# The first two pairs of weight tiles of the input projection: smaller loads from two queues, and a new order of the products

## The reference, cut to what matters

```python
    proj = jnp.einsum('btd,dc->btc', x, w_in) + b_in
    q, k, v, glu = jnp.split(proj, [ATTN_WIDTH, ATTN_WIDTH + KV_WIDTH, ATTN_WIDTH + 2 * KV_WIDTH], axis=-1)
    ...
    attn, new_k, new_v = attend_fn(q, k, v)
    a, g = jnp.split(glu, 2, axis=-1)
    c, new_conv = causal_dwconv(conv_hist, a * jax.nn.sigmoid(g), conv_w, conv_b)
    c = jax.nn.silu(layer_norm(c, conv_ln_g, conv_ln_b))
    mix = jnp.einsum('btm,md->btd', jnp.concatenate([attn, c], axis=-1), w_out) + b_out
    x = layer_norm(ALPHA * x + mix, ln1_g, ln1_b)
    h = jnp.einsum('btd,df->btf', x, ffn_w_up)
    h, new_ffn = causal_dwconv(ffn_hist, h, ffn_conv_w, ffn_conv_b)
    hu, hg = jnp.split(h, 2, axis=-1)
    f = jnp.einsum('btf,fd->btd', jax.nn.silu(hg) * hu, ffn_w_down)
    x = layer_norm(ALPHA * x + f, ln2_g, ln2_b)
```

## Time and profile before

| | us |
|---|---|
| median of 3 runs | 2038.24 |
| lowest, highest | 2037.86, 2039.66 |
| the profiled execution, its own time | 2040.65 |
| its span | 2039.1 |
| TensorE busy in the span | 1992.8 (98%) |
| first real product starts | 8.47 |
| second pair ends, first q product starts | 38.30 |

### The profile page before, as it was taken

The page is one execution under the profiler, slowest core; times in us unless marked ns, Lnnn a source line. Parts: engine busy times, 40 slices in busy tenths (PEclk is TensorE's granted clock), DMA queues, the critical chain, the costliest instruction groups (busy, mean ns, idle before and its releaser), DMA issues. The chain is left out here.

```text
span 2039.1 us, 42519 instructions
## 1 busy us (share of the span) xinstructions
PE 1992.8 (98%) x15699; PEld 1971.7 (97%) x15699; DVE 1660.6 (81%) x2619; ACT 990.4 (49%) x1503; POOL 408.0 (20%) x557
## 2 busy tenths in 40 slices
PE   8999999999998999999999999999999999999996
PEld 8999999899988999999999999999999999999995
DVE  3599899977699777777777777777778889899898
ACT  3445444433566454444444444444446545454445
POOL 0022223120642211111111121111211121112212
PEclk9999999999999999999999999999999999999997
DMA  6322222123657767667677676776766898779973
GB/s 223 99 78 78 84 88 77 51 81 127 204 156 217 206 180 187 181 183 194 176 186 191 177 191 175 185 191 176 188 179 206 227 239 219 200 204 229 219 178 118
DMA packets 123279, 344.03 MB, mean 169 GB/s; under 512 B 14420, under 2 KB 24932, under 8 KB 123168
## 3 DMA queue, kind: packets, MB, share of 16 engines
q1 hardware_dynamic: 94336, 260.40, 38.0%
q0 software_dynamic: 27824, 80.20, 23.0%
q10 hardware_dynamic: 1008, 1.93, 0.3%
HBM read 314.06 MB, written 23.97 MB: 166 GB/s over the span
## 5 line engine op out<-in xcount | busy, mean ns | idle before, releaser
L1021 PE MATMUL acc<-comb,w_hi 128*128 128x274 f32 x4784 | 917.9, 291 | 9.7 <-DVE comb L2180 7.6
L1021 PEld LDWEIGHTS acc<-comb,w_hi 128*128 128x128 f32 x4784 | 756.6, 189 | 11.3 <-DVE comb L2180 5.9
L1021 PE MATMUL acc<-comb,w_lo 128*128 128x274 f32 x2392 | 691.4, 289 | 0.0
L1021 PEld LDWEIGHTS acc<-comb,w_lo 128*128 128x128 f32 x2392 | 456.4, 191 | 0.0
L1138 PE MATMUL acc<-comb,w_hi 128*128 128x272 f32 x2240 | 424.4, 288 | 3.6 <-DVE w_lo L2321 3.0
L1138 PEld LDWEIGHTS acc<-comb,w_hi 128*128 128x128 f32 x2240 | 352.2, 189 | 5.9 <-DVE w_lo L2321 3.6
L1138 PE MATMUL acc<-comb,w_lo 128*128 128x272 f32 x1120 | 323.3, 289 | 0.0
L1428 ACT ACTIVATE w_hi<-sum 128x1024 fp32r<-128x1024 f32 x172 | 182.4, 1060 | 241.1 <-PE acc L1021 136.4
L2125 DVE TENSOR_TENSOR w_lo<-sum,w_hi 128x1024 fp32r<-128x1024 f32 x172 | 210.7, 1225 | 80.3 <-ACT w_hi L1428 75.7
L2125 DVE TENSOR_TENSOR w_lo<-raw_a,w_hi 128x1024 fp32r<-128x1024 f32 x125 | 152.8, 1222 | 100.5 <-ACT w_hi L1428 100.5
L1138 PEld LDWEIGHTS acc<-comb,w_lo 128*128 128x128 f32 x1120 | 210.9, 188 | 0.0
(11 more groups left out here) (306 smaller groups left out, 3171.2 us busy)
## 6 DMA issues: line engine op xcount, KB each, us to landing
raw_a<-w_up SPq DMA_DIRECT2D x127, 512.0 KB, 6.2
stage<-w_stream SPq DMA_DIRECT2D x90, 512.0 KB, 3.3
sum<-w_up POOLq DMA_DIRECT2D x89, 512.0 KB, 7.1
sum<-w_up SPq DMA_DIRECT2D x88, 512.0 KB, 3.3
d_a<-w_down SPq DMA_DIRECT2D x96, 320.0 KB, 4.6
act_spill<-prod_f SPq DMA_DIRECT2D x43, 272.0 KB, 5.9
d_s<-w_down SPq DMA_DIRECT2D x32, 320.0 KB, 4.4
d_s<-w_down POOLq DMA_DIRECT2D x32, 320.0 KB, 6.9
```

Of the source, the lines that this page charges most:

```text
L1021: mm = pe.matmul(bank(b), wt[:, k * P:(k + 1) * P], prod_comb(j, k, c), start=start and q == 0, stop=stop and q == 2, skip_group_check=True)
```

## The change

SP loads the first 512 columns of halves 0 and 1 by themselves (256 KB each), and the remaining columns of both in one transfer. ACT issues two x loads, tile 0 and tiles 2-3, ahead of everything else. The later x tiles come in loads of two, two, four and four tiles. Half 2 is loaded ahead of x tiles 8 to 15, and half 3 between tiles 8-11 and 12-15. Half 2 gets buffers of its own (`w_hi3`, `w_lo3`, which lie over the x tiles 0 to 3 of `x_raw`), so its cast no longer waits for PE to use up half 0. The casts of x are single tiles up to tile 5, then pairs. In the first pair PE takes two row tiles of each slot by turns, and slot 0 multiplies in the order hi·hi, lo·hi, hi·lo and waits for the high part alone at first. There are 11 warm-up products in place of 13.

```diff
-X_PART = 2
+X_LOADS = ((0, 1), (1, 2), (2, 4), (4, 6), (6, 8), (8, 12), (12, 16))
+X_PARTS = ((0, 1), (1, 2), (2, 3), (3, 4), (4, 5), (5, 6), (6, 8), (8, 10), (10, 12), (12, 14), (14, 16))
+X_NTH = (2, 3, 5, 6, 7, 8, 9, 10, 11, 12, 13)
-WARM_UP = 13
+WARM_UP = 11
...
+            def first_row_tile(a, k):
+                w = slice(k * P, (k + 1) * P)
+                for q, (wt, x) in enumerate(((w_hi, x_hi), (w_lo, x_hi), (w_hi, x_lo))):
+                    if q == 1 and k == 0:
+                        pe.wait_ge(part_lo, 1)
+                    if q == 2 and k in x_first:
+                        pe.wait_ge(part_lo, X_NTH[x_first.index(k)])
+                    for h, (c0, c1) in enumerate(X_CUT):
+                        mm = pe.matmul(acc[:, a, h, 0:c1 - c0], wt[:, 0, w], x[:, k, c0:c1], start=k == 0 and q == 0, stop=False)
...
-            LAG = (0, 0, 0) + (0, 1) * 5 + (1, 1, 1)
+            LAGS = ((0, 0, 1, 1) * 4, (0, 0, 0) + (0, 1) * 5 + (1, 1, 1))
...
+            act.wait_ge(w_loaded[0], 32)
+            act.wait_ge(part_lo, 6)
+            act.activation(first_hi(2), stage[:, 0, :], ACT.Copy).then_inc(hi_ready, 1)
+            x_part(6)
             act.dma_start(par[:, :], dram["params"]).then_inc(par_loaded, 16)
             act.dma_start(mask[:, :, :], dram["mask"]).then_inc(par_loaded, 16)
             act.dma_start(ident[:, :], dram["ident"]).then_inc(par_loaded, 16)
-            for i in range(2, KT // X_PART):
+            for i in range(7, len(X_PARTS)):
                 x_part(i)
-            prep(2, 0)
             prep(3, 1)
```

More of the change, by code:

```diff
@@ L451, in sem @@
             return ctx.enter_context(nc.semaphore(name))
-        x_loaded = [sem(f"x_loaded{i}") for i in range(KT // X_PART)]
+        x_loaded = [sem(f"x_loaded{i}") for i in range(len(X_LOADS))]
+        w_rest_loaded = sem("w_rest_loaded")
         w_loaded = [sem("w_loaded0"), sem("w_loaded1")]
@@ L514, in _ @@
             ws = dram["w_stream"]
-            load_half(0, 0, ws[0], first=True)
-            load_x(0)
+            load_half(0, 0, ws[0][:, 0:512], cols=512, first=True)
             load_x(1)
-            load_half(1, 1, ws[1], first=True)
-            for i in range(2, KT // X_PART):
-                load_x(i)
-            for n in range(2, 10):
+            load_half(1, 1, ws[1][:, 0:512], cols=512, first=True)
+            sp.dma_start(stage[:, :, 512:1024], ws[0:2, :, 512:1024].rearrange("n p c -> p n c")).then_inc(w_rest_loaded, 16)
+            load_x(3)
+            load_x(4)
+            load_half(2, 0, ws[2])
+            load_x(5)
+            load_half(3, 1, ws[3])
+            load_x(6)
+            for n in range(4, 10):
                 load_half(n, n % 2, ws[n])
@@ L763, in pair @@
                     k = done[slot]
[L764 removed]
+                    if k == (4 if n == 0 else 0):
                         pe.wait_ge(lo_ready, n + slot + 1)
@@ L767, in pair @@
                         ready(k)
-                    mm = row_tile(n, slot, accs[slot], k, k0 + k, rhs_hi, rhs_lo, cut, first and k == 0, last and k == nk - 1)
+                    if n == 0 and slot == 0:
+                        mm = first_row_tile(accs[0], k)
+                        done[0] += 1
+                        continue
+                    if n == 0 and k == 0:
+                        pe.wait_ge(part_lo, 4)
+                    mm = row_tile(n + slot, accs[slot], k, k0 + k, rhs_hi, rhs_lo, cut, first and k == 0, last and k == nk - 1)
                     done[slot] += 1
@@ L793, in _ @@
             for s in range(2):
-                pair(2 * s, (0, 1), x_hi, x_lo, X_CUT, 8 * s, LAG, lambda k, s=s: x_ready(8 * s + k), first=s == 0, last=s == 1)
+                pair(2 * s, (0, 1), x_hi, x_lo, X_CUT, 8 * s, LAGS[s], lambda k, s=s: x_ready(8 * s + k), first=s == 0, last=s == 1)
             def turn_v():
@@ L1173, in x_part @@
             def x_part(i):
[L1174 to L1176 removed]
+                act.wait_ge(x_loaded[[c1 >= X_PARTS[i][1] for _, c1 in X_LOADS].index(True)], 16)
+                c = slice(*X_PARTS[i])
+                act.activation(x_hi[:, c, :], x_raw[:, c, :], ACT.Copy).then_inc(part_hi, 1)
+            for i in (0, 2):
+                c = slice(*X_LOADS[i])
+                act.dma_start(x_raw[:, c, :], dram["xT"][:, c, :]).then_inc(x_loaded[i], 16)
             act.wait_ge(consts_set, 1)
             act.activation(soft[:, 0, 0:1], ones[:, 0, 0:1], ACT.Copy)
[L1180 removed]
+            act.wait_ge(w_loaded[0], 16)
+            act.activation(w_hi[:, 0, 0:512], stage[:, 0, 0:512], ACT.Copy).then_inc(part_hi, 1)
             x_part(0)
             x_part(1)
[L1183 removed]
+            act.wait_ge(w_loaded[1], 16)
+            act.activation(w_hi[:, 1, 0:512], stage[:, 1, 0:512], ACT.Copy).then_inc(part_hi, 1)
+            x_part(2)
+            x_part(3)
+            act.wait_ge(w_rest_loaded, 16)
+            for n in range(2):
+                act.activation(w_hi[:, n, 512:1024], stage[:, n, 512:1024], ACT.Copy).then_inc(hi_ready, 1)
+            x_part(4)
+            x_part(5)
+            act.wait_ge(w_loaded[0], 32)
+            act.wait_ge(part_lo, 6)
+            act.activation(first_hi(2), stage[:, 0, :], ACT.Copy).then_inc(hi_ready, 1)
+            x_part(6)
             act.dma_start(par[:, :], dram["params"]).then_inc(par_loaded, 16)
@@ L1194, in _ @@
             act.dma_start(mask_m[:, :], dram["mask_m"]).then_inc(att_loaded, 16)
+            act.wait_ge(w_loaded[0], 48)
+            act.wait_ge(half_used, 1)
+            act.activation(w_hi[:, 0, :], stage[:, 0, :], ACT.Copy).then_inc(hi_ready, 1)
             act.wait_ge(par_loaded, 48)
-            prep(4, 0)
+            act.wait_ge(half_used, 3)
             act.activation(halves(kT[:, PAD:KCOLS]), A(0), ACT.Identity, bias=pcol("b_k")).then_inc(k_ready, 1)
```

51 lines of the change are left out of this document (36 added, 15 removed).

## The result

| | before | changed |
|---|---|---|
| median of 16 runs, us | 2039.6 | 2042.97 |
| lowest, highest | 2037.86, 2040.91 | 2041.71, 2044.12 |
| ratio, 95% interval | | 1.0017 (1.0011 to 1.0024) |
| the profiled execution, its span | 2040.65, 2039.1 | 2041.71, 2040.1 |
| first real product | 8.47 | 6.40 |

The change makes the kernel 3.4 us slower, 0.17%. The forecast was 2037.6, a little faster, with a range up to 2039.6: wrong in sign and outside the range. 3.4 us lies inside the 0.2% that the forecast called "within", but the 16 runs of each tell it from nothing: the slowest run of before (2040.91) is faster than the fastest changed one. The forecast started from 2038.24, the median of the three runs known then; the median of 16 is 1.4 us higher.

The account below looks back on a forecast made before the run. PE, busy 98%, bounds the kernel, so the q blocks' start sets the time: last x landing 21.8 + 14.2 casts and row tiles + 1.7 clock = 37.7, 0.6 us earlier than 38.30, giving 2037.6 us; range 2034.4 to 2039.6.

Parts of the forecast that it names:

- The reading of the bound: Whole kernel: PE is busy 98% of the span, so an earlier start of the q blocks shifts the end equally.
- E: Moment PE goes on to the q blocks without a stop (first q product): 38.30 us before, forecast 37.7.
- The begin: Start of the kernel: PE's first real product at 6.3 us, 2.2 us earlier than 8.47.
- The first pair: Row tiles of weight halves 0 and 1: a 0.5 us stop for tiles 6-7, ending near 20.1 instead of 22.3.
- Half 2 is the next 512 KB, so it lands at about 13.6: Load of weight half 2 behind x tiles 6-7: 1.3 us at 411 GB/s, landing at about 13.6 us.
- L: Time at which the last x load (tiles 12 to 15) lands: forecast 21.8 us, bounds 20.2 and 23.1.
- The lagging engine: One DMA engine of 16 running behind the rest: may delay the last x load by 0 to 1.2 us.
- The last of it cannot arrive much earlier than now, in whatever order: Loads of the stage, 4 weight halves and x: busy DMA engines leave the last arrival about where it was.
- The small loads: Parameters, mask and identity, 692 KB: most share with the last x load, landing it at 21.0 us (20.2 to 22.0).
- The wait that takes the place of the gap: PE idle in front of half 3's first row tile, from 23.2 to 26.7 us: 3.5 us.
- The clock: Lower PE clock behind the idle time in front of half 3: a loss of 1.7 us.
- Rival (3): Small loads ahead and lagging engine on the last x load make it slower: 2038.9 to 2039.9 us, chance 0.17.

Follow-up runs that it names:

- e4: Changed kernel with x tile 0 and tiles 2-3 issued by SP in order of need instead of by ACT; median 2043.95 us, ratio 1.0021 to before.
- e1: Changed kernel with raw halves 2 and 3 loaded into buffers of their own, so SP does not wait before issuing them; median 2041.07 us.
- e8: Kernel before the change with loads of parameters, mask and identity issued behind the cast of half 3 instead of half 1; median 2037.33 us, ratio 0.9990.
- e3: Changed kernel with loads of parameters, mask and identity (692 KB) issued behind the last x cast; median 2041.05 us, ratio 1.0006 to before.
- e6: Changed kernel with 16 more products of constants in front of half 3's first row tile, filling PE's stop; median 2040.36 us, ratio 1.0004 to before.
- e2: Changed kernel with half 3's casts put ahead of the casts of x tiles 12 to 15 on ACT and DVE; median 2037.86 us, ratio 0.9991 to before.
- e7: Changed kernel with the first pair's old order of row tiles and of the three terms; median 2039.96 us, ratio 1.0004 to before.
- e9: Changed kernel with 36 warm-up products of 40 x 40 in place of 11 of 128 x 128; median 2043.07 us, ratio 1.0017 to before.

## Why the prediction was wrong, point by point

- **The reading of the bound** (98% PE; E carries over to the end) held to within 1.5 us in all profiles. What stands behind E took 2000.8 us before and 1999.95 after the change.
- **The begin**: PE starts at 6.40, forecast 6.3, and that is luck. The forecast's 6.3 was the end of the warm-up, with the high parts ready at 5.7. In the trace the 22 warm-up records took 4.56 us, not 5.0, and ended at 5.8; PE then waited 0.6 us for the high part of x tile 0. The step "about the same bytes, so again about 4.5" was off: half 0's piece was cast at 5.16, since 116 and then 303 GB/s were moved in 2 to 4 us, where the kernel before had 242 and 386. I had taken the rate from whole loads; the new begin loses 0.6 us of supply (e4 shows that the number of queues is not the cause).
- **The first pair**: forecast to end at 20.1, it ended at 21.5 (22.3 before). "0.9 us for the lower clock and one wait" was 2.1 by 18.4 us, at a granted clock of 1.00 all the time: the one wait, for half 1's piece, left PE idle for 1.1 us and cost 1.4 by the starts of the products around it. The stop for the low part of tiles 6-7 was in its place, 0.4 us long, forecast 0.5.
- **"Half 2 is the next 512 KB, so it lands at about 13.6"** is the step that failed. It landed at 15.2; without the wait at its issue (e1) it is cast at 14.05, so 1.1 of the 1.6 us are that wait. I counted its bytes and left out its issue: SP waits there for half 0's low part, which before was done at 6.8 and is now at 11.8, because the second columns of half 0 are the fourth piece on the queue. The loads in flight ran out at 12. And with half 2 everything behind it on SP's queue was held, both four-tile loads. e1 prices it: 1.4 us of L, 1.9 us of the median. I had the row (the wait for `lo_ready` in the order of SP) and didn't put a time to it.
- **L, first "21.0" and with the lagging engine 21.8**: fifteen of the 16 parts were in at 23.0. Of the 2.0 us, 1.4 are the dry queue (e1) and the other 0.6 fit the slow start's 0.26 MB.
- **The lagging engine, "0 to 1.2 us", taken as 0.8**: 1.5, above its bound. It was seen in the rows before, where it is 1.2 and goes with an instruction transfer at 19.0; a load of all four last tiles in one makes PE wait for its latest part.
- **"The last of it cannot arrive much earlier than now, in whatever order"**: true of the order, but the 692 KB of small loads are not needed in this stage. In e8, without them, the last half is in at 21.4 instead of 23.1.
- **The small loads** beside the last x: 1.2 us by e3, inside the two bounds.
- **The wait that takes the place of the gap**: right in place, chain and form (4.9 us from L to the low part; 12 row tiles). Its size was 4.7 instead of 3.5: L was 2.7 us late, and PE came to it 1.5 us late, at 24.7 instead of 23.2.
- **The clock**: 1.7 forecast, 1.4 in the profile, and up to 2.7 in others; e6 gives 2.6 us in the median, where its own profile shows 1.4 by the clock and 0.2 by an earlier L.
- **Rival (3)** was the right one by its condition, L above 22.4, but its price stopped at L = 23.1. Its longest case was also added up wrong: 37.3 and twice 1.7 are 40.7, not 40.0, which makes 2040.6 us. The range should have had a term for a queue that runs dry.
- **The start of the sum**: with the measured E of 40.15 it gives 2038.24 + 1.85 = 2040.1 us, already above the range. Of the 2.9 us to 2042.97, 1.4 are the median of three runs that it started from, and the rest is the open point below.

What stays open: the medians differ by 3.4 us, the two profiles' E by 1.85 and their spans by 1.0. The changed kernel's profiled execution was the fastest of its 16 and the one before among its slower ones. The clock's loss behind the stop differs between the profiles of the changed kernel and its variants by 1.3 us and would explain much of it, but no profile of a typical execution of both was compared.

## What to carry to other kernels

When a load is moved forward on a queue, put a time to the wait in front of its issue, and add up what else stands behind it; bytes by rate is only the lower bound. An engine's earlier start is worth nothing until the last item of the stage comes earlier: follow the last landing through every instruction that stands behind it on each engine, and see first whether something that isn't needed yet can leave the supply (e8, three lines) or whether the work that doesn't need the last item can go ahead of it (e2, one line moved per engine). Look also at what follows a stop: the lower clock behind it costs time where PE goes straight on to the end of the stage (the changed kernel, 1.4 us), and none where a wait would have followed anyway (e7, as I read it).

## What the runs showed of the hardware

- A transfer of 16 KB of instructions takes one DMA engine 0.9 to 1.1 us, and the loads queued then complete 1.1 to 1.9 us late in one of their 16 parts, on to the end of the backlog. Each whole load then completes that late.
- The same loads cut in smaller pieces, in another order, moved 1.16 MB by 6 us instead of 1.42, with one queue or two.
- One issue of a transfer on SP took 1.41 us instead of 0.43 while such an instruction transfer ran (e9; once).
- A stop of PE of 4.7 us was followed by a clock of 0.58 in the next 3.6 us. With products of constants in it (e6) the clock stayed at 1.00, with the wait's end 0.2 us away. Behind each of the other stops of 2.0 to 5.1 us in this stage the granted clock of the next 3 to 5 us was 0.50 to 0.61; behind the stops of 1.0 to 1.3 us it stayed at 1.00.
- The price of that lower clock for 12 row tiles varied from 1.4 to 2.7 us in six profiles with stops of 3.4 to 5.1 us.
